# Softmax weights of six attention units turned through DRAM and VectorE instead of on TensorE

## The reference

```
s = jnp.einsum('bqkgd,bskd->bkgqs', qblk, k).astype(jnp.float32) * scale
p = jax.nn.softmax(s, axis=-1).astype(v.dtype)
return jnp.einsum('bkgqs,bskd->bqkgd', p, v)
```

## Time and profile before

| | us |
|---|---|
| median of 3 runs | 2854.54 |
| the profiled execution, its own time | 2853.88 |
| its span in the trace | 2852.6 |
| TensorE busy | 2828.6 (99%) |
| VectorE busy | 1827.6 (64%) |
| ScalarE busy | 1441.7 (51%) |
| GpSimd busy | 137.0 (5%) |
| granted TensorE clock, mean | 0.999 |
| moved by DMA | 655.10 MB, 230 GB/s |

### The profile page before, as it was taken

One profiled execution on the slowest core, in us unless ns is written; L12 is line 12 of the kernel. 1 busy time (PEld: TensorE's weight loads), 2 busy tenths in 40 slices (PEclk: granted clock), 3 DMA queues, 4 the chain that ended last, 5 costly groups with the idle time before them and its releaser, 6 DMA issues. The chain is left out here.

```text
span 2852.6 us, 34813 instructions
## 1 busy us (share of the span) xinstructions
PE 2828.6 (99%) x13510; PEld 2344.8 (82%) x13510; DVE 1827.6 (64%) x2287; ACT 1441.7 (51%) x1959; POOL 137.0 (5%) x213
## 2 busy tenths in 40 slices
PE   9999999999999999999999999999999999999998
PEld 8888888887888878888888888888888888888887
DVE  6577777777755757567555555556656556666557
ACT  5456666555554655444443434434545545645544
POOL 1100000000000000000000000000000020000110
PEclk9999999999999999999999999999999999999999
DMA  7878888888877879775675655656586667766665
GB/s 258 253 253 269 275 284 278 283 285 267 255 228 235 254 222 299 237 254 157 216 212 177 199 175 191 204 175 201 165 274 210 209 211 218 234 224 222 218 218 184
DMA packets 376738, 655.10 MB, mean 230 GB/s; under 512 B 63981, under 2 KB 87389, under 8 KB 375550
## 3 DMA queue, kind: packets, MB, share of 16 engines
q1 hardware_dynamic: 271104, 510.33, 55.8%
q10 hardware_dynamic: 91278, 98.36, 11.1%
q0 software_dynamic: 14192, 44.20, 4.5%
HBM read 603.05 MB, written 49.74 MB: 229 GB/s over the span
## 5 line engine op out<-in xcount | busy, mean ns | idle before, releaser
L1657 DVE TENSOR_TENSOR w_lo<-raw,w_hi 128x1024 fp32r<-128x1024 f32 (+2 forms) x976 | 1154.4, 1205 | 664.6 <-ACT w_hi L1010 656.2
L978 PE MATMUL bank<-w_lo,x_hi 128*128 128x512 f32 (+2 forms) x3888 | 1525.2, 392 | 10.1 <-DVE w_lo L1657 6.9
L980 PE MATMUL bank<-w_hi,x_lo 128*128 128x512 f32 (+2 forms) x3888 | 1508.3, 388 | 0.0
L979 PE MATMUL bank<-w_hi,x_hi 128*128 128x512 f32 (+2 forms) x3888 | 1507.2, 388 | 0.0
L1010 ACT ACTIVATE w_hi<-raw 128x1024 fp32r<-128x1024 f32 (+2 forms) x976 | 992.5, 1045 | 764.1 <-PE bank L980 274.1
L978 PEld LDWEIGHTS bank<-w_lo,x_hi 128*128 128x128 f32 x3888 | 730.6, 188 | 164.0 <-issue 11.0
L980 PEld LDWEIGHTS bank<-w_hi,x_lo 128*128 128x128 f32 x3888 | 730.2, 188 | 150.4
L979 PEld LDWEIGHTS bank<-w_hi,x_hi 128*128 128x128 f32 x3888 | 730.8, 188 | 147.5 <-issue 2.9
L1020 ACT ACTIVATE x_hi<-bank 128x512 fp32r<-128x512 f32 (+1 forms) x96 | 52.8, 588 | 271.2 <-PE bank L659 261.2
L1668 DVE TENSOR_TENSOR x_lo<-bank,x_hi 128x512 fp32r<-128x512 f32 (+1 forms) x96 | 61.7, 674 | 154.2 <-ACT x_hi L1020 154.2
L2461 POOL DMA_DIRECT2D proj<-stage x48 | 34.5, 718 | 2163.7 <-DVE stage L2326 1454.4
(11 more groups left out here) (224 smaller groups left out, 1293.0 us busy)
## 6 DMA issues: line engine op xcount, KB each, us to landing
raw<-in_w_in SPq DMA_DIRECT2D x492, 512.0 KB, 5.0
raw<-in_w_up SPq DMA_DIRECT2D x128, 512.0 KB, 4.1
raw<-in_w_down SPq DMA_DIRECT2D x128, 512.0 KB, 4.6
raw<-in_w_out SPq DMA_DIRECT2D x96, 512.0 KB, 4.8
arena<-proj ACTq DMA_DIRECT2D x74, 512.0 KB, 5.3
raw<-in_w_ssd_branch SPq DMA_DIRECT2D x64, 512.0 KB, 5.6
proj<-stage POOLq DMA_DIRECT2D x48, 512.0 KB, 5.7
raw<-in_w_gla_branch SPq DMA_DIRECT2D x32, 512.0 KB, 5.3
```

The source lines that it names most:

```text
L978: pe.matmul(o, x_hi[:, xk, tokens(t)], w_lo[:, r, k, 0:b.n], start=a, stop=False)
L979: pe.matmul(o, x_hi[:, xk, tokens(t)], w_hi[:, r, k, 0:b.n], start=False, stop=False)
L980: op = pe.matmul(o, x_lo[:, xk, tokens(t)], w_hi[:, r, k, 0:b.n], start=False, stop=z_)
L1657: TT(w_lo[:, p % SPLIT_RING, 0:b.per, 0:b.n], raw[:, p % RAW_RING, 0:b.per, 0:b.n], w_hi[:, p % SPLIT_RING, 0:b.per, 0:b.n].bitcast(F32), ...
```

## The change

For the units "a" 0, "a" 1 and "b" 0 of both layers, `BY_DRAM` takes the place of `ATTEND`. GpSimd waits for the exponentials of a query tile and stores its 128x1024 weights with `turned_store`, now in four DMAs of 128 KB, to a DRAM scratch of its own; tile 1 follows. At steps 4 and 5 ScalarE waits for the store of tile 0 and of tile 1 and issues the read back, over the same SBUF room. At step 6 VectorE waits for both reads and turns the 32x32 blocks of each tile into `pts[0]` and `pts[1]` (tile 1 uses the room of the turned queries or keys, free by then). TensorE's transposes and ScalarE's copies go for these units. Values are at steps 7 and 8 (from 5 and 7), output at 10 (from 9). The neighbourhood unit stays. In `gpsimd`, the sends of a layer's blocks are split so that those drained before a unit's exponentials are issued ahead of that unit's stores and the others behind.

```diff
+BY_DRAM = {"exp": 1, "turn0": 3, "back0": 4, "back1": 5, "turned": 6, "values0": 7, "values1": 8, "out": 10}
-def turned_store(dma, to, tile, signal):
+def turned_store(dma, to, tile, signal, n=S // SQUARE):
-    for b in range(S // SQUARE):
+    for b in range(n):
...
+    probs_by_key = {(l, *name): [scratch(f"probs{l}{''.join(map(str, name))}{t}",
+                                         [UNIT_H * S // SQUARE, SQUARE, P // SQUARE, SQUARE]) for t in range(NT)]
+                    for l in range(LAYERS) for name in (("a", 0), ("a", 1), ("b", 0))}
...
+            self.pts = [self.pt, self.qt]
...
             def times_values(t):
                 if key[1] == "c":
                     pe.wait_ge(*load[0]["unit", *key])
-                pe.wait_ge(*unit.act["pt", *key, t])
+                    pe.wait_ge(*unit.act["pt", *key, t])
+                else:
+                    pe.wait_ge(*unit.dve["pt", *key, t])
...
+            else:
+                yield at + BY_DRAM["values0"]
+                times_values(0)
+                yield at + BY_DRAM["values1"]
+                times_values(1)
+                yield at + BY_DRAM["out"]
...
             fetch_gate(key, gate, gate_col)
-            take_probs(0)
-            yield at + ATTEND["values0"]
-            act.wait_ge(*unit.pe["values", *key, 0])
-            take_probs(1)
+            if by_dram:
+                for t in range(NT):
+                    yield at + BY_DRAM[f"back{t}"]
+                    act.wait_ge(*probs_out[t][key])
+                    act.dma_start(probs[t], turned_rows(probs_by_key[key][t])).then_inc(*probs_in[t](*key))
...
+            if steps is BY_DRAM:
+                yield at + steps["turned"]
+                for t in range(NT):
+                    dve.wait_ge(*probs_in[t][key])
+                    turn(flat(pts[t]), flat(probs[t])).then_inc(*unit.dve("pt", *key, t))
...
+        def probabilities(key, probs):
+
+            for t in range(NT):
+                pool.wait_ge(*unit.act["exp", *key, t, 3])
+                turned_store(pool.dma_start, probs_by_key[key][t], flat(probs[t]).unsqueeze(1),
+                             lambda: probs_out[t](*key), P // SQUARE)
+
         for l in range(LAYERS):
-            sends([b for b in sent if b.info[0] in ("proj2", "latent") and b.info[-1] == l])
+            begin = start_of["latent_in", 0, l].first + UNIT_FIRST + UNIT_STEP["scores"] + BY_DRAM["exp"]
+            of_layer = [b for b in sent if b.info[0] in ("proj2", "latent") and b.info[-1] == l]
+            early = lambda b, n: b.last + DRAIN < begin + n * UNIT_PACE
+            sends([b for b in of_layer if early(b, 0)])
+            probabilities((l, "a", 0), ga.probs)
+            sends([b for b in of_layer if early(b, 1) and not early(b, 0)])
+            probabilities((l, "a", 1), ga.probs)
+            sends([b for b in of_layer if early(b, 2) and not early(b, 1)])
+            probabilities((l, "b", 0), lu.probs)
+            sends([b for b in of_layer if not early(b, 2)])
```

More of the change, by code:

```diff
@@ L476, in emit @@
     gate_in = tally("gate_in", 16)
+    probs_out = [tally(f"probs{t}_out", 16) for t in range(NT)]
+    probs_in = [tally(f"probs{t}_in", 16) for t in range(NT)]
     total_in = tally("total_in", 16)
@@ L817, in turn_heads, with attend @@
             op.then_inc(*unit.pe(*key))
-        def attend(key, at, q_of, k_of, value, probs, pt, gate, rotated=None):
+        def attend(key, at, q_of, k_of, value, probs, pts, gate, rotated=None):
             yield at
@@ L877, in grouped @@
             yield from attend(key, UNIT_STEP["scores"], lambda h: ga.qt[:, h, :], lambda h: ga.kt[:, 0, :],
-                              lambda h, kt: ga.v[:, kt, :], ga.probs, ga.pt, ga.gate)
+                              lambda h, kt: ga.v[:, kt, :], ga.probs, ga.pts, ga.gate)
         def latent_unit(l):
@@ L1459, in attend @@
             exponentials(1)
+            by_dram = key[1] != "c"
             yield at + ATTEND["turn0"]
             fetch_gate(key, gate, gate_col)
-            take_probs(0)
-            yield at + ATTEND["values0"]
-            act.wait_ge(*unit.pe["values", *key, 0])
-            take_probs(1)
+            if by_dram:
[3 more added lines that the diff above has]
+                    act.dma_start(probs[t], turned_rows(probs_by_key[key][t])).then_inc(*probs_in[t](*key))
+            else:
+                take_probs(0)
+                yield at + ATTEND["values0"]
+                act.wait_ge(*unit.pe["values", *key, 0])
+                take_probs(1)
             act.wait_ge(*gate_in[key])
@@ L1468, in attend @@
                 A(gate[:, t, :], gate[:, t, :], ACT.Silu).then_inc(*unit.act("gate", *key, t))
-            yield at + ATTEND["out"]
+            yield at + (BY_DRAM if by_dram else ATTEND)["out"]
             for t in range(NT):
@@ L2196, in with_gain, with attend @@
             op.then_inc(*unit.dve("sin", l, name))
-        def attend(key, at, probs, scale, bias, gate, x0):
+        def attend(key, at, probs, pts, scale, bias, gate, x0):
             yield at
@@ L2239, in attend @@
             one_over_sums(1)
-            yield at + ATTEND["values0"]
+            steps = ATTEND if key[1] == "c" else BY_DRAM
+            if steps is BY_DRAM:
[3 more added lines that the diff above has]
+                    turn(flat(pts[t]), flat(probs[t])).then_inc(*unit.dve("pt", *key, t))
+            yield at + steps["values0"]
             gates(0)
-            yield at + ATTEND["values1"]
+            yield at + steps["values1"]
             gates(1)
-            yield at + ATTEND["out"]
+            yield at + steps["out"]
             for t in range(NT):
@@ L2272, in grouped @@
             dve.wait_ge(*unit.act["root", *key, "q"])
-            yield from attend(key, UNIT_STEP["scores"], ga.probs, None, None, ga.gate, KT + 4 * u)
+            yield from attend(key, UNIT_STEP["scores"], ga.probs, ga.pts, None, None, ga.gate, KT + 4 * u)
         def latent_unit(l):
@@ L2289, in latent_unit @@
                      lambda a: wide(a, [P, 2, B_ROPE]))
-            yield from attend(key, UNIT_STEP["scores"], lu.probs, QW ** -0.5, None, lu.gate, KT + A_H)
+            yield from attend(key, UNIT_STEP["scores"], lu.probs, lu.pts, QW ** -0.5, None, lu.gate, KT + A_H)
         def neighbour(l):
@@ L2304, in neighbour @@
             dve.wait_ge(*unit.dve.now)
-            yield from attend(key, UNIT_STEP["scores"], nu.probs, HD ** -0.5,
+            yield from attend(key, UNIT_STEP["scores"], nu.probs, nu.pts, HD ** -0.5,
                               nu.bias.rearrange("p t (h n) -> p t h n", h=C_H), nu.gate, KT + A_H + B_H)
```

28 lines of the change are left out of this document (16 added, 12 removed).

## The result

The changed kernel takes 2893.3 us (median of four runs, 2889.3 to 2894.1), the kernel before 2853.8 beside it: ratio 1.0135, 95% interval 1.012 to 1.015. It is 39 us slower, where 2847.7 was forecast and 2862 was the end of the range. The profiled execution took 2889.3 us, the fastest of the four.

The account below looks back on a forecast made before the run. The attention layers were taken as bound by TensorE's own work. From the 2854.5 us median, 10.4 us of removed transposes less 3.6 given back made 2847.7 us; range 2843.5 to 2862.

Parts of the forecast that it names:

- Removed transposes, 10.4 us: TensorE, attention layers: 12 groups of eight transposes leave the path at 0.87 us each, 10.4 us gained, nothing hidden.
- The 275 ns each of the Trainium skill: TensorE's 96 removed transposes at the skill page's price: 26 us gained, about 2832 us; given no chance.
- Issue of 0.72 us: GpSimd's eight stores per unit: 0.72 us for each issue, low bound 0.65, the last starting at 2171.6.
- The rival with 1.31: GpSimd's stores: an issue costs 1.31 us by its pieces, every unit stalls, 28.2 us together, 2872.3 us; chance 0.20.
- From last issue to landing, 5.1 us (to 5.7): GpSimd's store of tile 1: in DRAM 5.1 us after its last issue, at 2176.7 (from 2174.8 to 2177.3).
- the late store: Rival on GpSimd's stores: late by their issue price, 1.31 us each, stalling every unit; 2872.3 us, chance 0.20.
- The Trainium skill's rule on pieces under 512 B: Stores in 128 B pieces: DMA engines read, modify and write under 512 B, which speaks against the change; about 2878 us.
- The chain behind the landing, 6.6 us: ScalarE's read issue, gate work and conversion, then VectorE's conversion and turn of tile 0: 6.6 us with hand-offs.
- Read back 4.4 us, never last: Tile 0's read from DRAM: 4.4 us, in by about 2178.8, so not the last thing waited for.
- Given back, 3.6 us: TensorE's stalls at values 0: 0.5 us per grouped unit, 0.8 per latent unit, 3.6 in all (0 to 7.2).
- Output a step later, 0 (at worst 4.6): Next unit's start: output at step 10 costs 0, room of 1.4 and 1.75 us holds; at worst 4.6 us.
- these engines' stops do not reach the weight stream: ScalarE and VectorE waits: conversions are four steps (10.9 us) ahead, the longest new stop some 6 us, so no cost.

## Why the prediction was wrong

The sum was -6.8 us. Measured were +39.5 between the medians and +35.4 between the profiled spans; the split below is of the spans. The kernel with GpSimd's read and values at step 9 has the same TensorE instructions and no stops, so it splits that. Work removed: 2828.6 - 2820.0 = 8.6 us. Slow clock: 2832.5 - 2820.0 = 12.5. Idle: 55.5 - 24.0 = 31.5. Together -8.6 + 12.5 + 31.5 = 35.4. Busy times of two executions are good to a microsecond or two. Read from the trace itself, TensorE works 23.0 us at 0.50 behind the six stops, which costs it 11.5, 1.9 for each; a short stretch at 0.50 near 38 us, far ahead of the layers changed, adds 1.7.

- **Removed transposes, 10.4 us:** 8.6 by the account above, the right size. The 1.8 us that are missing can be chance: the kernel before and the one with its output a step later do the same TensorE work and show 2828.6 and 2829.6, and of the former 1.7 are a stretch at 0.50 near 706 us that the latter has not. The 275 ns each of the Trainium skill ("TensorE: Matmul & The Clock Gate", Part 4: PE-mode transpose), 26 us, hold as the duration of one (a mean of 273 in the group of line 842 before) and not as what its removal gains.
- **Issue of 0.72 us:** 0.787 was measured, so 0.2 us more from the last exponential to the last issue. The rival with 1.31 was right that the store is late, but not by its issues.
- **From last issue to landing, 5.1 us (to 5.7):** this is the step that failed. It was 10.8 in the first unit and 8.7 to 10.3 in the others. The error was to take a median over single issues: the wait ends with the last of eight, and within the burst the landings went from 5.0 to 10.8 us. I had worked out what twice my 5.1 would do, 2878 us, and given it no more than a part of the late store's 0.20; with the 12.5 us of slow clock it comes to some 2891, near the 2893.3 measured. The Trainium skill's rule on pieces under 512 B ("DMA: Bandwidth & Descriptors", Specifications) pointed the right way: on GpSimd's queue whole rows took 17 us off the waits. On ScalarE's queue the same pieces landed in 3.4 to 4.4 us, so the pieces alone are not the cause, and what in GpSimd's queue makes the last one late is open.
- **The chain behind the landing, 6.6 us:** 2187.48 - 2181.22 = 6.3. Right, but not the only thing that was late, for:
- **Read back 4.4 us, never last:** tile 0's took 11.1 to 13.0 us. In the changed kernel it was in 0.4 us ahead of its use; with the gate work moved, or the store in whole rows, it was last. The same mistake: the row of heads_y came from another stretch.
- **Given back, 3.6 us:** 30.7. In the first unit from the last exponential's start (2166.13) to the values 21.4 us, forecast 2183.3 - 2167.54 = 15.8. The difference of 5.6 is 0.2 for the issues, 5.7 for the landing and -0.3 behind it.
- **Clock, not in the sum:** 11.5 to 12.5 us, about 2 for each stop. The first one shows it directly: 3.43 - 1.70 = 1.73 us in the values, and from the next matmul's start to the one after 0.56 (2190.91 to 2191.47), not 0.32 as behind values 1, another 0.24.
- **Output a step later, 0 (at worst 4.6):** no longer wait at the head transposes by its own run, and 0 to 5 us of time. But "these engines' stops do not reach the weight stream" held only for weights: with the values moved to step 9 the stops of 3.6 to 6.6 us at steps 4 and 5 (or VectorE's behind them) reached the next unit's head transposes, 7.9 us in four places.
- **The range** took the late store to 2862 from the issue price alone; the bound that mattered, the landing of the last piece, had gone into it with 0.6 us. The slow clock had not gone into it at all.

Left open: how much of tile 0's read is its neighbours in the queues, and whether ScalarE or VectorE held up the next units.

## What to carry to other kernels

Price a round trip over DRAM by the last landing of the burst, here 8.7 to 10.8 us, not by the median of single transfers in quieter stretches (4.7 to 5.7), and the read beside the burst in the same way. Add to a stop of TensorE the slow clock behind it: all six stops of 4.2 to 6.0 us had it, and with stops of 1.7 to 3.1 us (GpSimd's read, steps 7 and 8) four of six. Try the wait and the read on an engine that has nothing else due: moving them from ScalarE to GpSimd was worth 21 to 28 us, by a sooner read and by a ScalarE that does not stand, and only together with two later steps did it make the change a gain.

## What was not expected of the hardware

- TensorE's clock was 0.50 in the values behind each stop of 4.2 to 6.0 us (3.2 to 3.4 us, not 1.7), in three of six only from about the stop's end on, which made a stop cost about 2 us more than its length.
- In a burst of eight 128 KB stores from GpSimd (first unit) the first landed 5.0 us after its issue and the last 10.8.
- The same stores had a median landing of 6.2 to 6.8 us when GpSimd issued them and of 3.5 when ScalarE's queue did, but at 0.3 to 2.8 us of ScalarE's time for each issue, against 0.79 of GpSimd's.
- A store of 128 KB cost 0.79 us to issue in 128 B pieces and 0.49 in 4 KB rows.
- A 512 KB read took 9.7 us (median) in 512 B pieces and still 8.3 in whole rows, where a read of 1 KB pieces in another stretch took 4.4. Tile 0's took 11.1 to 13.0 us from ScalarE's queue and 7.9 to 9.8 from GpSimd's.
